# Gathering the tokens of an expert with fp32 products in place of three bf16 parts

## The reference

```python
logits = xn @ w_router + b_router                 # 256 tokens, 32 experts
top_val, top_idx = lax.top_k(logits, 4)
gates = softmax(top_val)
for each expert e:                                # its tokens xb = xn[tok]
    h = xb @ w_gate_up[e] + b_gate_up[e]          # 1024 -> 2048
    hact = (clip(u) + 1) * (min(g, 7) * sigmoid(1.702 * min(g, 7)))
    out[tok] += gate * (hact @ w_down[e] + b_down[e])   # 1024 -> 1024
```

## Time and profile before

| | us |
|---|---|
| median of three executions | 1311.43 |
| lowest, highest | 1308.37, 1311.65 |
| profiled execution | 1306.64 |
| its span, first to last instruction | 1304.7 |
| TensorE busy (of the span) | 1192.7 (91%) |
| its weight loads busy | 616.2 (47%) |
| VectorE busy | 484.2 (37%) |
| ScalarE busy | 248.9 (19%) |
| DMA, from HBM | 459.76 MB, 353 GB/s over the span |

### The profile page before, as it was taken

The page is one execution under the profiler, slowest core; times in us unless marked ns, Lnnn a source line. Parts: engine busy times, 40 slices in busy tenths (PEclk is TensorE's granted clock), DMA queues, the critical chain, the costliest instruction groups (busy, mean ns, idle before and its releaser), DMA issues.

```text
span 1304.7 us, 18542 instructions
## 1 busy us (share of the span) xinstructions
PE 1192.7 (91%) x7533; PEld 616.2 (47%) x7533; DVE 484.2 (37%) x744; ACT 248.9 (19%) x350; POOL 5.6 (0%) x10
## 2 busy tenths in 40 slices
PE   6996999999799999999999989899999989899996
PEld 6986998998543333333333333333333333333332
DVE  6846866655422223222222222222222222222224
ACT  5427644534400001000010010000010010000011
POOL 0000100000000000000000000000000000000000
PEclk9998999999989999999999999999999999999998
DMA  8523564552979999999999999999999999999991
GB/s 316 190 97 154 208 206 154 192 186 104 398 327 414 428 430 427 427 430 428 427 429 429 427 429 429 427 429 428 428 428 430 428 428 429 428 428 428 429 427 54
DMA packets 36526, 461.26 MB, mean 354 GB/s; under 512 B 4224, under 2 KB 4240, under 8 KB 5392
## 3 DMA queue, kind: packets, MB, share of 16 engines
q1 hardware_dynamic: 36000, 459.82, 84.7%
q0 software_dynamic: 208, 0.54, 0.2%
q10 hardware_dynamic: 288, 0.46, 0.1%
HBM read 459.76 MB, written 1.05 MB: 353 GB/s over the span
## 4 chain that ended last, share of the span: by engine, by line
DMA 52%; PE 43%; DVE 2%; ACT 1%; issue 1%; SPq 0%; ACTq 0%; DVEq 0%
DMA late<-in_w_gate_up 51%; PE ps L1225 17%; PE ps L1100 5%; PE ps L1101 5%; PE ps L1102 5%; PE ps L1119 2%; PE ps L1121 2%; PE ps L1120 2%; PE ps L1135 1%; PE ps L1276 1%; PE ps L1250 1%; DMA raw<-in_dense 1%; ACT whi L420 1%; PE ps L1284 1%; PE ps L1185 1%
## 5 line engine op out<-in xcount | busy, mean ns | idle before, releaser
L1225 PE MATMUL ps<-late,s 128*64 128x512 f32 x1128 | 515.4, 600 | 65.8 <-DMA late<-in_w_gate_up 64.9
L1226 PE MATMUL ps<-late,s 128*64 128x512 f32 x1128 | 515.4, 600 | 0.0
L1225 PEld LDWEIGHTS ps<-late,s 128*64 128x64 f32 x1128 | 143.6, 137 | 392.3 <-issue 255.1
L987 DVE TENSOR_TENSOR res<-res,ps 128x1024 f32<-128x1024 f32 x66 | 80.6, 1221 | 267.7 <-PE ps L1276 267.7
L1100 PE MATMUL ps<-act_hi,whi 128*128 128x256 f32 x576 | 163.6, 284 | 1.5 <-DVE act_lo L661 1.5
L1101 PE MATMUL ps<-act_lo,whi 128*128 128x256 f32 x576 | 163.0, 283 | 0.0
L1102 PE MATMUL ps<-act_hi,wlo 128*128 128x256 f32 x576 | 163.0, 283 | 0.0
L577 ACT ACTIVATE s<-ps 128x512 f32<-128x512 f32 x64 | 34.7, 594 | 571.7 <-PE ps L1226 571.7
L1226 PEld LDWEIGHTS ps<-late,s 128*64 128x64 f32 x1128 | 143.6, 137 | 0.0
L680 DVE TENSOR_TENSOR wlo<-raw,whi 128x2048 fp32r<-128x2048 f32 x48 | 110.0, 2294 | 73.6 <-ACT whi L420 73.4
L1226 PE MATMUL ps<-raw,s 128*64 128x512 f32 x272 | 123.9, 598 | 0.0
(11 more groups left out here) (175 smaller groups left out, 985.9 us busy)
## 6 DMA issues: line engine op xcount, KB each, us to landing
late<-in_w_gate_up SPq DMA_DIRECT2D x125, 2048.0 KB, 25.5
raw<-in_w_down SPq DMA_DIRECT2D x32, 2048.0 KB, 25.6
raw<-in_dense SPq DMA_DIRECT2D x51, 1024.0 KB, 4.8
late<-in_w_down SPq DMA_DIRECT2D x16, 2048.0 KB, 25.3
s<-in_w_down SPq DMA_DIRECT2D x16, 2048.0 KB, 25.3
raw<-in_w_gate_up SPq DMA_DIRECT2D x2, 2048.0 KB, 10.8
s<-in_w_gate_up SPq DMA_DIRECT2D x1, 2048.0 KB, 13.5
res<-in_x SPq DMA_DIRECT2D x2, 512.0 KB, 5.3
```

The source lines that it names most:

```text
L987: V.tensor_tensor(res[:, t, :], res[:, t, :], ps[:, OUT_BANK[t]:OUT_BANK[t] + 2, :].rearrange("p b n -> p (b n)"), ALU.add)\
L1225: nc.tensor.matmul(ps[0:SLOTS, bank, :], x_tile, lower, start=start, stop=stop)
L1226: return nc.tensor.matmul(ps[SLOTS:P, bank, :], x_tile, upper, start=start, stop=stop)
```

## The change

The normalised rows are kept whole in fp32, `xn32`, written by one ScalarE instruction for each block of 128 tokens (`scaled_rows`, in the place of `high_rows`). The one-hot is fp32 as well. A gather is then two products for each block of 128 features, 16 in place of 48. `middle_rows`, `rest_rows_of` and `low_rows` are gone, and with them three semaphores. The four seeds of VectorE move from just ahead of its loop to the start of its program, behind its first two memsets.

```diff
-        half = [s[:, :].bitcast(BF16) for s in (s2, s3)]
-        n16 = TT * D
-        xpart = [v.rearrange("p (t d) -> p t d", d=D)
-                 for v in (half[0][:, 0:n16], half[0][:, n16:2 * n16], half[1][:, 0:n16])]
-        onehot = half[1][:, n16:n16 + TT * SLOTS].rearrange("p (t c) -> p t c", c=SLOTS)
+        xn32 = rows(s2)
+        onehot = s3[:, 0:TT * SLOTS].rearrange("p (t c) -> p t c", c=SLOTS)
...
-            def high_rows(t):
+            def scaled_rows(t):
                 act.wait_ge(S["rstd_done"], t + 1)
-                nc.scalar.activation(xpart[0][:, t, :], res[:, t, :], ACT.Copy, scale=rstd[:, 6 + t:7 + t])\
-                    .then_inc(S["part_hi"], 1)
-
-            def middle_rows(t):
-                act.wait_ge(S["part_rest"], t + 1)
-                nc.scalar.activation(xpart[1][:, t, :], rest_rows[:, t, :], ACT.Copy).then_inc(S["part_mid"], 1)
+                nc.scalar.activation(xn32[:, t, :], res[:, t, :], ACT.Copy, scale=rstd[:, 6 + t:7 + t])\
+                    .then_inc(S["rows_scaled"], 1)
...
-            middle_rows(0)
...
-            high_rows(1)
-            middle_rows(1)
+            scaled_rows(1)
...
             seq[0] += 2
+            dve.sem_inc(S["wone_turned"], 1)
+            dve.sem_inc(S["out_done"], 1)
+            dve.sem_inc(S["added"], 2)
+            dve.sem_inc(S["x_ready"], 1)
             dve.wait_ge(S["in_cst"], 32)
...
-            rest_rows_of(0)
             evacuate("xnT", 3, copied(xn_f))
-            low_rows(0)
             inverse_root(1)
...
-            rest_rows_of(1)
...
             select(0, 0)
-            low_rows(1)
...
-            dve.sem_inc(S["wone_turned"], 1)
-            dve.sem_inc(S["out_done"], 1)
-            dve.sem_inc(S["added"], 2)
-            dve.sem_inc(S["x_ready"], 1)
             n = needed_rounds(dve)
...
                 for k in range(KT):
-                    for n in range(3):
-                        for t in range(TT):
-                            last = nc.tensor.matmul(ps[:, 5, k * SLOTS:(k + 1) * SLOTS],
-                                                    xpart[n][:, t, k * P:(k + 1) * P], onehot[:, t, :],
-                                                    start=n == 0 and t == 0, stop=n == 2 and t == TT - 1)
+                    for t in range(TT):
+                        last = nc.tensor.matmul(ps[:, 5, k * SLOTS:(k + 1) * SLOTS], xn32[:, t, k * P:(k + 1) * P],
+                                                onehot[:, t, :], start=t == 0, stop=t == TT - 1)
                 last.then_inc(S["sel_done"], 1)
...
-            pe.wait_ge(S["part_hi"], TT)
-            pe.wait_ge(S["part_mid"], TT)
-            pe.wait_ge(S["part_low"], TT)
+            pe.wait_ge(S["rows_scaled"], TT)
             select(0, 0)
```

More of the change, by code:

```diff
@@ L257, in build @@
             lam_abs lam_exp pads_zero xr_done pool_done decay_done inner_done mult_done scan_done
-            gelu_arg gelu_sig yb_done m_done lam_done rowmax prob_done part_hi part_rest part_mid part_low
+            gelu_arg gelu_sig yb_done m_done lam_done rowmax prob_done rows_scaled
             rstd_done router_scaled gmat_zero gate_in gate_exp picked gmat_done gT_turned gT_out bd_done bd_added route_done
@@ L541, in _ @@
             added_up = lambda t: (S["freed_dve"], evacuated(UNIT["o"] + 2 * t + 1)[1])
-            def high_rows(t):
+            def scaled_rows(t):
                 act.wait_ge(S["rstd_done"], t + 1)
-                nc.scalar.activation(xpart[0][:, t, :], res[:, t, :], ACT.Copy, scale=rstd[:, 6 + t:7 + t])\
-                    .then_inc(S["part_hi"], 1)
-            def middle_rows(t):
-                act.wait_ge(S["part_rest"], t + 1)
-                nc.scalar.activation(xpart[1][:, t, :], rest_rows[:, t, :], ACT.Copy).then_inc(S["part_mid"], 1)
+                nc.scalar.activation(xn32[:, t, :], res[:, t, :], ACT.Copy, scale=rstd[:, 6 + t:7 + t])\
+                    .then_inc(S["rows_scaled"], 1)
             square(6, res[:, 0, :], xn_rows[:, 0, :], added_up(0))
-            high_rows(0)
+            scaled_rows(0)
             for j in range(3):
@@ L864, in inverse_root @@
                 V.reciprocal(rstd[:, 6 + t:7 + t], root[:, 6 + t:7 + t]).then_inc(S["rstd_done"], 1)
[L866 to L875, removed]
             for j in range(3):
```

## The result

The changed kernel takes 1316.98 us in the median of five executions (1316.47 to 1319.57), the kernel before 1310.13 us beside it. The ratio is 1.0057, 95% interval 1.0042 to 1.0071: slower by 0.57%, some 7.5 us, where +3 us were forecast. The profiled executions, 1316.47 and 1306.64 us, have spans 9.7 us apart.

A forecast was written before the change was run, and what follows sets the result against it. Transfers bound the late loop (29.4 us an expert against TensorE's 26.4). First gather -2.0, second +2.1, third +0.8, last +2.1 sum to +3.0 us, so 1311.4 becomes 1314.4 us; range 1310 to 1320.

The forecast's parts named there:

- The bound, the gaps, the lag: Expert loop: transfers set the late pace, idle gaps and tail decide the time; TensorE's first weight wait moves to near 870 us.
- (1) Seeds and parts: Head: without count, seeds and part-making ahead of it, the first gather starts 4.2 us earlier, at 354.0.
- (2) The gather: Each gather: 32 instructions at 0.11 us, 3.67 us warm; D, the extra time per gather, is +2.1 us.
- rival A: Expert loop: loads and columns add up (0.16 us), TensorE becomes the bound, +43 us, 1354 us; chance 0.08.
- (3) Second, third and last gather: Around expert 1 and in the tail: longer gathers cost 2.1, 0.8 and 2.1 us where exposed.
- (3) First gather: Head: 4.9 us including 1.2 for the low clock, ending at 358.9 instead of 360.93, a gain of 2.0 us.
- Rival B: Half clock throughout the first gather (+5.4 us in all), or pace 0.115 to 0.12 us (+3.7 to +4); chance 0.30.

The follow-up runs named there:

- run 7: Kernel before with its head and first gather unchanged, fp32 gather in the 32 others: ratio 1.0043, 5.6 us slower than the kernel before.
- run 2: Kernel before with only VectorE's four seeds moved to the program's start: ratio 1.0014 to the kernel before.
- runs 9 to 11: run 9, run 10, and the kernel before with seeds first, unread products in all idle stretches and eight more between weighted-bias products: ratio 0.9967.
- run 9: Changed kernel with fillers (products nobody reads) in all idle stretches around the head and expert 1: ratio 1.0004 to the kernel before, median 1310.4 us.
- run 10: Kernel before, seeds in their old place, with fillers (products nobody reads) in idle stretches around the head and expert 1: ratio 0.9962.
- run 8: Changed kernel with the one-hot cut to its first 32 columns in each product, slots above left out: 1346.35 us in one execution.
- run 6: Changed kernel with rows and one-hot in bf16, one part only, two lower parts left out: ratio 0.9939 to the kernel before, median 1301.7 us.

## Why the prediction was partly right

*The bound, the gaps, the lag.* Right. Transfers at 429 GB/s set the late pace before and after, and the time is decided where they stand idle and in the tail. TensorE's first wait was put near 870 us and came at 917.

*(1) Seeds and parts, 4.2 us earlier.* Right: 354.19 against 354.0. The one-hot ends at 354.1 and the gather follows.

*(2) The gather, D = +2.1.* Right in count (32 instructions) and in what sets it: 3.79 us warm (at full clock) against 3.67, D = 2.2. The load time by the Trainium skill, page "TensorE: Matmul & The Clock Gate", section "LDWEIGHTS (loading the stationary operand)", fits: 107 ns for 128 columns stand beside (3.65 - 0.19) / 31 = 0.112 us from loads of the changed kernel:

```profile
1277.95 3.65 PEld L1225 LDWEIGHTS ps<-s 128*128 128x128 f32 x32 [0.81 <-issue]
```

If such loads did not overlap products, as in rival A, the pace would have been 0.16 and TensorE the bound; neither the pace nor the time shows it.

*(3) Second, third and last gather, +5.0 together.* Right: +2.2, +0.5, +2.2 in the profiles. The loop alone cost 5.6 us in run 7, but with the clock's 1.7 us around expert 1 in it, which the sum had as unchanged.

*(3) First gather, a gain of 2.0.* This step failed. It reads "the clock will have fallen, or fall as it starts ... I take 1.2 us again", that is, the clock would return after 2.7 us of the gather as in the earlier trace rows. It returned after 13.7 us. The gather took 7.0 us instead of 4.9, and expert 0's first chunks, priced at nothing, lost 2.8 us; in place of -2.0 stood +3.1 against the profile before. Rival B had the first half of this (+5.4 in all) at a chance of 0.30; no rival had the second half. Rival B's other way, a pace of 0.115 to 0.12 us, adds 0.6 to 0.9 to the sum of 3.0, so +3.6 to +3.9 and not +3.7 to +4.

The mistake was to take one return of the clock, from one profile of a bf16 gather, as the price. That gather's 2.72 us were already the price of half clock throughout: run 2's, with the clock at 0.50 in all windows from 358 to 366 us, takes as long.

```profile
359.70 2.72 PE L1250 MATMUL ps<-s 128*128 128x64 bf16 x48 [3.38 <-DVE s L878]
```

So the 1.2 us carried over belonged to a whole gather of 1.57 us at half clock, not to an early return, and for one of 3.67 us it was too little.

The kernel before is itself hit in many executions, which is why the medians lie 7 us apart and the two profiles 9.7. Of its 27 executions beside runs 9 to 11, the two whose mean granted clock was that of its profile, 0.988, took 1305.7 and 1306.3 us, and the sixteen with 0.982 to 0.984 took 1309.9 to 1312.4. Set against a head so hit (run 7), the change costs 1.1 us at the first issue, 3.9 to expert 1's, 0.5 and 2.2: 7.7 in all, beside the 7.5 measured.

With the fillers in both, run 9 against run 10 is 1.0004 to 0.9962, or 5.5 us: the fp32 gather costs this much even with its head 1.8 us earlier at the first issue. The terms at full clock are -1.8 + 2.2 + 0.5 + 2.2 = +3.1. Of the rest some 1.2 us are the clock's fall around expert 1 in run 9 (12.0 us from the second gather's end to expert 1's issue, against 10.8 in run 10); what is left is within the two intervals. So the change's price without the clock lies between 3 us, by its terms, and 5.5, by the times.

The chances: 0.38 on slower by over 0.3% and 0.55 on within it, where slower came. The range, 1310 to 1320, held 1317, but partly by luck: its upper end stood there for a slower pace of the loads and 2 us of spread, and what filled it was the clock.

## What to carry to other kernels

Before counting products, count weight loads: a product with few columns costs its load, and 16 fp32 products are 32 slow loads where 48 bf16 ones are 48 fast ones. When TensorE has little work ahead of a critical stretch (nearly 5 us here, and the clock fell), price that stretch and what follows it at half clock, not only until the first return seen in a profile. Products put in the idle stretches were worth 5 us in the kernel before (run 10) and some 7 in the changed one (run 9), about as much as the change itself, 7.5. And read how many microseconds an expert is away from the next bound: 0.8 us here, and four more products a gather, 0.9 us, cost 17 us.

## What the runs showed of the hardware that had not been expected

TensorE was at work and its clock stayed low. In the changed kernel it ran loads and products without a pause from 354.2 to 361.2 us, and the granted clock stayed 0.50 until 367.9. In run 8, with 32 columns instead of 64 behind the same loads, the clock fell again and again inside a loop in which TensorE was busy 25 of 25 us, and the one execution took 29 us more:

```profile
500.00:525.00 25.00, 25.00 (x126) 10.62 (x124) 6.51 (x13) 2.20 (x4) 0.00 (x0) 0.93 1.00 427
```

In the stretch read closely, the fall came at 449.0 us, 0.6 us behind the end of a gather at full clock (444.65 to 448.41 us).

A low mean clock does not by itself mean a slow kernel. In run 6 it was 0.971, below every other kernel but run 8's, and the median, 1301.7 us, was the lowest of all; TensorE's products waited 75.7 us for weights there.

The dense stage ahead, the same code in all of these kernels, ended up to 4 us apart in the profiles (344.7 to 348.9 us). Differences in the head were readable only from a common mark within it.
